# Third layer's gate products: standing token rows and streaming gate weights, tile by tile

## The reference

```python
def deltanet_layer(x, valid, g_norm, w_in, conv_w, a_log, dt_bias, o_gain, w_out):
    h = jnp.where(valid[None, :, None], rms_norm_2(x, g_norm), 0)
    z = h @ w_in                       # 1024 -> 4*1024 + 16 columns
    qkv = jax.nn.silu(causal_dwconv(z[..., :2 * DN_KW + DN_VW], conv_w))
    ...
    b_raw = z[..., 2 * DN_KW + 2 * DN_VW:2 * DN_KW + 2 * DN_VW + DN_HEADS].astype(jnp.float32)
    a_raw = z[..., 2 * DN_KW + 2 * DN_VW + DN_HEADS:].astype(jnp.float32)
    ...
    beta = jax.nn.sigmoid(b_raw)
    g = -jnp.exp(a_log.astype(jnp.float32)) * jax.nn.softplus(a_raw + dt_bias.astype(jnp.float32))
```

## Time and profile before

| | |
|---|---|
| median of 3 runs | 3046.01 us |
| lowest and highest of them | 3044.57 and 3047.44 us |
| the profiled execution's own time | 3046.62 us |
| its span, from first to last instruction | 3044.8 us |
| PE busy | 2942.3 us, 97% of the span |
| DVE, ACT, POOL busy | 1490.8, 800.5 and 451.9 us |
| mean granted TensorE clock | 0.987 of 2.4 GHz |

### The profile page before, as it was taken

How to read it: one execution, slowest core, us unless ns; L and a number is a source line. 1 busy time by engine, 2 the same in 40 slices (tenths; PEclk the granted TensorE clock), 3 DMA queues, 4 the chain that set the end, 5 groups by cost and what they waited for, 6 DMA issues and landing times. The chain is left out here.

```text
span 3044.8 us, 38916 instructions
## 1 busy us (share of the span) xinstructions
PE 2942.3 (97%) x15011; PEld 1851.6 (61%) x15011; DVE 1490.8 (49%) x3493; ACT 800.5 (26%) x2061; POOL 451.9 (15%) x753
## 2 busy tenths in 40 slices
PE   5999999999999999799999999999799999999999
PEld 2445555555555554588787887754688888544454
DVE  2344544645545443556656566534355656344441
ACT  1113333333333331212323323221222222021230
POOL 0221221312213000120201102000001111111100
PEclk8999999999999999899999999999899999999999
DMA  7340001100013200421121211401511111030101
GB/s 250 127 150 28 28 28 39 45 28 28 28 56 90 76 1 14 143 70 45 53 77 36 77 49 49 164 23 49 146 36 49 29 30 56 1 126 15 55 1 55
DMA packets 137439, 186.78 MB, mean 61 GB/s; under 512 B 22284, under 2 KB 90540, under 8 KB 135204
## 3 DMA queue, kind: packets, MB, share of 16 engines
q1 hardware_dynamic: 136056, 184.21, 19.1%
q10 hardware_dynamic: 1200, 0.09, 0.0%
HBM read 174.61 MB, written 9.67 MB: 61 GB/s over the span
## 5 line engine op out<-in xcount | busy, mean ns | idle before, releaser
L488 PE MATMUL a_psP<-a_w,a_uT 128*128 128x512 f32 x1536 | 699.5, 600 | 6.3 <-DMA a_w<-a_w_in 6.3
L488 PEld LDWEIGHTS a_psP<-a_w,a_uT 128*128 128x128 f32 x1536 | 280.3, 191 | 323.3 <-issue 323.3
L737 DVE TENSOR_REDUCE a_small<-a_psS 128x1 f32<-128x768 f32 (+1 forms) x192 | 140.8, 775 | 401.7 <-PE a_psS L516 401.7
L1460 PE MATMUL b_psP<-b_w,b_uT 128*128 128x256 f32 x768 | 184.0, 382 | 0.7 <-DVE b_raw L1743 0.3
L643 ACT ACTIVATE a_e<-a_psS,a_small 128x768 f32<-128x768 f32 (+1 forms) x192 | 144.0, 754 | 139.0 <-DVE a_small L737 138.6
L1460 PEld LDWEIGHTS b_psP<-b_w,b_uT 128*128 128x128 f32 x768 | 141.9, 190 | 23.5 <-issue 3.7
L1780 DVE TENSOR_REDUCE b_small<-b_psS 128x2 f32<-128x512 f32 x64 | 44.3, 692 | 213.0 <-PE b_psS L1517 213.0
L650 ACT COPY a_pT<-a_psS 128x768 f32<-128x768 f32 (+1 forms) x96 | 63.1, 657 | 311.2 <-PE a_psS L525 311.2
L538 PEld LDWEIGHTS a_psO<-a_v,a_pT 128*128 128x128 f32 x896 | 115.1, 192 | 45.9 <-issue 45.9
L1617 ACT ACTIVATE b_e<-b_psS,b_small 128x512 f32<-128x512 f32 x128 | 86.8, 683 | 192.0 <-DVE b_small L1793 190.1
L1624 ACT COPY b_e<-b_psS 128x512 f32<-128x512 f32 x128 | 71.9, 587 | 228.4 <-PE b_psS L1527 147.3
(11 more groups left out here) (490 smaller groups left out, 5104.4 us busy)
## 6 DMA issues: line engine op xcount, KB each, us to landing
a_w<-a_w_in SPq DMA_DIRECT2D x16, 2048.0 KB, 9.1
b_w<-b_w_in SPq DMA_DIRECT2D x48, 512.0 KB, 3.8
a_yT<-mod_w SPq DMA_DIRECT2D x8, 1536.0 KB, 8.4
a_yT<-mod_w SPq DMA_DIRECT2D x8, 1024.0 KB, 19.0
b_yT<-b_w_in SPq DMA_DIRECT2D x16, 512.0 KB, 3.7
f_place<-bias_table SPq DMA_DIRECT2D x64, 128.0 KB
f_place<-a_w_in SPq DMA_DIRECT2D x16, 512.0 KB, 6.8
d_w<-a_w_in SPq DMA_DIRECT2D x16, 512.0 KB, 6.7
```

The costliest lines, as they stand in the source:

```text
L488: ins = nc.tensor.matmul(s.psP[:, x % 2, :], s.uT[:, a, t * P:(t + 1) * P], w[:, a, :], start=(a == 0), stop=(a == KD - 1))
L737: nc.vector.tensor_reduce(self.nm[i % 2][:, k:k + 1], self.score_banks(k, keys), AX_X, ALU.max, negate=True).then_inc(self.mx, 1)
L1460: ins = nc.tensor.matmul(out, lhsT, rhs, start=(a == 0), stop=(a == 3))
```

## The change

Five things are changed. The gate products are made tile by tile: a tile of `uT` stands (128 features x 128 tokens, 16 tokens for tile 0), and the 16 columns of the gate weights stream; the outcome lies at once with tokens on partitions, where `gates_T` had put it (PSUM bank 7). They are 40 matmuls in place of 16. The products of tile t-1 stand behind the transposes of tile t, and those of the last tile behind the taps. ACT's two copies are left out. `gates_T` is left out of the projections. The load of `wba` is issued before `h[2]` to `h[4]` and no longer after the taps.

```diff
-        names_t = ["xT%d" % t for t in range(CH)] + ["taps", "ba", "gates_T", "sums"]
+        names_t = (["xT0"] + sum([["xT%d" % t, "ba%d" % (t - 1)] for t in range(1, CH)], []) +
+                   ["taps", "ba%d" % LT, "sums"])
...
+        sp.dma_start(self.wba, a["a_w_in_2"][0][:, 4 * D:4 * D + 16].rearrange("(a p) n -> p a n", p=P)).then_inc(self.wba_in, 16)
         for t in range(2, CH):
             sp.dma_start(self.h[t], self.src(t)).then_inc(self.h_in[t], 16)
         sp.dma_start(self.taps, a["a_conv_2"][0]).then_inc(self.taps_in, 16)
-        sp.dma_start(self.wba, a["a_w_in_2"][0][:, 4 * D:4 * D + 16].rearrange("(a p) n -> p a n", p=P)).then_inc(self.wba_in, 16)
...
+        def gate_rows(t):
+            if t == 0:
+                pe.wait_ge(self.wba_in, 16)
+            pe.wait_ge(ve.sem, ve.at("uT%d" % t))
+            if t:
+                pe.wait_ge(ac.sem, ac.at("uT%d" % t))
+            for b in range(KD):
+                ins = nc.tensor.matmul(s.ps[0:chunk_len(t), 7, t * 16:(t + 1) * 16], s.uT[:, b, chunk_cols(t)],
+                                       self.wba[:, b, :], start=(b == 0), stop=(b == KD - 1))
+            te.done(ins, "ba%d" % t)
+
+        rows_T(0)
+        for t in range(1, CH):
+            rows_T(t)
+            gate_rows(t - 1)
         pe.wait_ge(self.taps_in, 16)
         ...
-        for k in range(2):
-            for b in range(KD):
-                ins = nc.tensor.matmul(s.ps[0:16, 5 + k, 0:m], self.wba[:, b, :], s.uT[:, b, k * m:(k + 1) * m],
-                                       start=(b == 0), stop=(b == KD - 1))
-        te.done(ins, "ba")
+        gate_rows(LT)
...
-        act.wait_ge(te.sem, te.at("ba"))
-        m = TOK // 2
-        nc.scalar.copy(self.gates[:, 0:m], s.ps[0:16, 5, 0:m])
-        ac.done(nc.scalar.copy(self.gates[:, m:2 * m], s.ps[0:16, 6, 0:m]), "gates")
...
-    def gates_T(self, pe):
-        nc, s, ac, te = self.nc, self.s, self.ac, self.te
-        pe.wait_ge(ac.sem, ac.at("gates"))
-        pe.wait_ge(self.ve.sem, self.ve.at("memsets"))
-        for t in range(CH):
-            ins = nc.tensor.transpose(s.ps[0:chunk_len(t), 7, t * 16:(t + 1) * 16], self.gates[:, chunk_cols(t)],
-                                      s.ident[0:16, 0:16])
-        te.done(ins, "gates_T")
...
-        dve.wait_ge(te.sem, te.at("gates_T"))
+        dve.wait_ge(te.sem, te.at("ba%d" % LT))
...
-                    if hp == 0 and self.PIECE.get(g) == 0:
-                        self.prepare.gates_T(pe)
```

More of the change, by code:

```diff
@@ L2020, in __init__ @@
         names_a = (["sq%d" % t for t in range(4)] + ["uT1", "sq4"] + ["uT%d" % t for t in range(2, CH)] +
-                   ["gates", "beta_tanh", "exp_x", "exp_alog", "ln", "eg", "edec", "egl"])
+                   ["beta_tanh", "exp_x", "exp_alog", "ln", "eg", "edec", "egl"])
         names_v = (["memsets", "identity16", "xn0", "xn1", "uT0"] + sum([["xn%d" % (t + 1), "uT%d" % t] for t in range(1, LT)], []) +
@@ L2040, in __init__ @@
         self.wba = s.kd[:, 0, 0:KD * 16].rearrange("p (a n) -> p a n", a=KD)
-        self.gates = s.kd[0:16, 1, 0:TOK]
         h2_rows = h2.rearrange("(t p) d -> t p d", p=P)
@@ L2074, in tensor, with rows_T @@
         nc, s, ve, ac, te = self.nc, self.s, self.ve, self.ac, self.te
-        for t in range(CH):
+        def rows_T(t):
             n = chunk_len(t)
@@ L2088, in tensor @@
         te.done(ins, "taps")
-        pe.wait_ge(self.wba_in, 16)
-        pe.wait_ge(ve.sem, ve.at("uT%d" % LT))
-        pe.wait_ge(ac.sem, ac.at("uT%d" % LT))
-        m = TOK // 2
-        for k in range(2):
-            for b in range(KD):
-                ins = nc.tensor.matmul(s.ps[0:16, 5 + k, 0:m], self.wba[:, b, :], s.uT[:, b, k * m:(k + 1) * m],
-                                       start=(b == 0), stop=(b == KD - 1))
-        te.done(ins, "ba")
+        gate_rows(LT)
         pe.wait_ge(ve.sem, ve.at("cw"))
```

## The result

The changed kernel takes 3054.35 us (median of 12 runs, 3048.98 to 3062.02), against 3045.57 us for the kernel before in the same sessions (12 runs, 3042.91 to 3053.79). The ratio is 1.0024, 95% interval 1.0015 to 1.0033: slower, by 7 to 9 us. The forecast was 3056.3 us, slower by over 0.2%, in a range of 3045.0 to 3058.5.

The account below looks back on a forecast made before the run. PE's own order was taken to bound the kernel, in the opening from 2149.61 on. First projection +8.4, slow projections +2.4, `gates_T` -0.45 made +10.3 us: 3056.9 against the profiled execution, 3056.3 as median; range 3045.0 to 3058.5.

Parts of the forecast that it names:

- the question whether the clock rises: In the opening, ahead of the projections: the clock was expected to stay at 1.2 GHz until the projections stream.
- Rival 1: Opening: unbroken loads and short products raise the clock at about 2154.4 as before; 3045.7 us, chance 0.26.
- Rival 3: Gate products: clock stays low but loads don't feel it, four tiles cost 7.2 us; 3049.9 us, chance 0.06.
- The products: Gate products of tiles 1 to 4 at 1.2 GHz: 3.41 us a tile, 13.6 us for four.
- The transposes: PE's transposes of three tiles at 1.2 GHz, from tile 2's start: 1.73 us a tile, 5.2 us together.
- The taps: 24 taps ahead of the last tile's gate products, at 0.11 us each: 2.6 us.
- The loads: Gate weights' 1024 small pieces, now ahead of the rows of tiles 2 to 4, delay tile 2's transposes 1.2 us.
- Rival 4: Loads: the small pieces hold the rows back longer than 1.6 us; over 3058 us, chance 0.05.
- The slow projections: First projections begin at the low clock: 2.4 us lost, bounds 1.7 to 3.5 us.
- `gates_T`: Small transposes removed from among the projections: 0.45 us saved, bounds 0.36 to 0.58 us.
- Tile 0's products: Tile 0's 16 records fit ahead of tile 2's transposes: at most 0.11 us each, 1.8 us.
- The forecast's case: Clock stays at 1.2 GHz through the opening until projections stream: 3056.3 us, reaching from 3054.5 to 3058, chance 0.56.

Follow-up runs that it names:

- the wide stream: Changed kernel with each gate product streaming the 16 weight columns eight times over (128 columns): 3044.85 us, 0.9999 to the kernel before.
- the products behind the taps: Changed kernel with all five tiles of gate products behind the taps, so the transposes stand in one run: 3060.81 us, 1.0046.
- the narrow products with a warm start: Changed kernel with 16 idle matmuls put into PE's waits in the opening: 3052.78 us, 1.0023 to the kernel before.
- the two kernels with a delay: Kernel before with 8 or 16 idle matmuls of 128 columns behind `gate_sums`: 3048.24 us (1.0009) and 3048.65 us (1.0014).
- one product in eight: Changed kernel with only the first of each tile's eight gate products, the others left out: 3041.56 us, 0.9984 to the kernel before.
- the wide stream with a warm start: Changed kernel with 128-column streams except tile 0's 16 columns, plus 16 idle matmuls in PE's waits: 3046.78 us, 1.0001 to the kernel before.

## Why the prediction was right

The step that carried it was the question whether the clock rises. In the profiled execution it did not, until the projections streamed; the wide stream takes the whole loss back (0.9999), and the products behind the taps and the narrow products with a warm start show the clock falling on them. Rival 1, an unbroken row of loads and short products that brings the clock, falls with these. Rival 3, loads that don't feel the clock, falls by the 333 ns of L2093 at 1.2 GHz against the 192 ns of its wide form at 2.4 GHz; the formula of the Trainium skill's "TensorE: Matmul & The Clock Gate", section "LDWEIGHTS (loading the stationary operand)", holds at the full clock (0.11 us a record, as said) and not at the low one (0.21 us). The rule of its "Part 4: PE-mode transpose", that transposes don't bring the full clock, is contradicted once more: with the products behind the taps the clock rose at 2152.6 on transposes alone, and it was lost 1.3 us into real matmuls.

The prediction read the clock's rise before at 2154.4, the edge of its stretch; the trace has it at 2154.8, which changes no case by more than 0.2 us.

Term by term:

- The products: 3.41 us a tile forecast, 3.27, 3.27, 3.37 and 3.44 measured. The transposes: 1.73, measured 1.74 to 1.76. The taps: 2.6, measured 2.64.
- The loads: this step was wrong. I had tile 2's transposes 1.2 us late; they came 3.24 us after tile 1's, before 3.10, and counted from the first transpose 5.67 us after it, before 5.28: no more than 0.4 us late, and the same distance was 4.93 us with the load alone moved, and 5.15 and 5.47 us in the two kernels with a delay, where nothing is changed ahead of it. SP did stall: the issue of the three loads of rows took 3.26 us and not 1.54. But it stalled behind the first of the three, which is tile 2's, and its rows were there at 2146.80, before at 2146.72. Rows of the changed kernel in order of time, SP's issues first and then ACT's squares of tile 2:

```profile
2140.36 0.58 SPq L2055 DMA_DIRECT2D d_kd<-a_w_in  x1
2140.99 3.26 SPq L2057 DMA_DIRECT2D g_rows<-h  x3
```

```profile
2146.80 1.06 ACT L2117 ACTIVATE d_ck<-g_rows 128x1024 f32<-128x1024 f32 x1 [2.08 <-DMA g_rows<-h]
```

  The nearest row that I took the earlier trace rows was of pieces that had nothing else to make way for. Rival 4 falls with it.
- The slow projections: 2.4 us forecast. From the first one to `gate_sums` it was 15.71 us, and 14.24 us in the kernel with wide streams: 1.5 us, under the 1.7 that I had as the lower end.
- `gates_T`: 0.45 us forecast. The same 14.24 us against 14.90 before make it 0.66 us, the whole of what the broken stream showed and a little more.
- Tile 0's products, which I bounded by 1.8 us, took 0.6 us with their tail.

The forecast's case was said to reach from 3054.5 to 3058 us (its terms add up to 3054.7 and 3057.9). The measured 3054.35 lies just under it, inside the stated range, which was drawn wide enough to hold rival 1 too. The opening was forecast at +10.3 us and was +8.1: of the 2.2 us between them, 0.8 are the loads', 0.9 the slow projections', 0.2 `gates_T`'s, and 0.3 those of the row from tile 2's transposes to the first projection (21.2 us against 21.5). Two more parts came that I hadn't in the sum: the layer began 0.3 us earlier, and behind `gate_sums` the profiled execution lost 2.9 us, of which one more low-clock spell is a part. In the profiled execution that adds up to +10.7 us; by the medians the whole is +8.8 us. That the miss in the opening and the loss behind it nearly cancel is luck.

## What to carry to other kernels

Before small and large operand change places in a matmul, count what streams as well as what it costs: 16 columns against a standing 128x128 f32 tile are paced by the load, and on this chip they also took the clock with them, while the profile showed PE busy at 100%. Read the granted clock beside the busy time, and where PE must do narrow work, let it stream wide, even on copies: here that cost nothing where the load is of 128 columns (1.78 us a tile wide, 1.70 narrow at the full clock) and gave back 7.6 to 9.5 us. A gain of 2 or 3 us in an opening is no gain until the rest of the kernel has been looked at, since the time behind it, and ahead of it, moved by as much.

## What the runs showed of the hardware

- The clock falls on busy work: 1.3 us after narrow matmuls' start in one kernel, behind 1.6 us of taps, from 1.00 to 0.50, with PE and PEld both busy for 12.10 of 12.10 us afterwards. With one product in eight it fell at the end of the taps.
- The clock rose on f32 transposes alone: at 2154.8 in the kernel before, after nothing but transposes since 2144.33.
- A load of 128 f32 columns lasts 192 ns at 2.4 GHz and 333 ns at 1.2 GHz; with loads of 16 columns, 16 records took 0.61 us with their tail.
- The same code, 866 us of it, took from 865.5 to 874.1 us in 14 traces, and its length followed the time at 1.2 GHz (14.7 to 34.1 us). No version with the whole work in it beats the kernel before for certain: the two best, the wide stream (0.9999, 0.9990 to 1.0008) and the wide stream with a warm start (1.0001, 0.9993 to 1.0010), are level with it, although their openings are 1.2 and 3.4 us shorter.
